# Hybrid decoder step on one core: moving the gate products of one prompt tile from the prologue of mixing into its position 0

## What is computed

```python
u = rmsnorm(x, norm_mix) @ w_in            # q, k, v | conv channels | z | a, b
o_swa = sliding-window attention with sinks (8 heads of 64, window 128)
o_gdn = chunked gated delta rule (8 heads of 64): triangular solve per chunk, state carried on
o_gdn = o_gdn * rsqrt(mean(o_gdn**2) + EPS) * gdn_norm_w * silu(z)
h = x + concat(o_swa, o_gdn) @ w_out
y = rmsnorm(h + hierarchical_moe(rmsnorm(h, norm_ffn)), norm_final)
```

## Time and profile before

| | us |
|---|---|
| median of 3 runs | 2289.5 (2286.6 to 2290.79) |
| the profiled execution, time | 2287.02 |
| the profiled execution, span | 2285.2 |
| PE busy (share of the span) | 2168.0 (95%) |
| DVE busy | 1296.6 (57%) |
| POOL busy | 612.7 (27%) |
| ACT busy | 548.6 (24%) |

### The profile page before, as it was taken

One profiled execution on the slowest core, in us unless ns is written; L12 is line 12 of the kernel. 1 busy time (PEld: TensorE's weight loads), 2 busy tenths in 40 slices (PEclk: granted clock), 3 DMA queues, 4 the chain that ended last, 5 costly groups with the idle time before them and its releaser, 6 DMA issues. The chain is left out here.

```text
span 2285.2 us, 47478 instructions
## 1 busy us (share of the span) xinstructions
PE 2168.0 (95%) x18764; PEld 1176.5 (51%) x18764; DVE 1296.6 (57%) x2674; ACT 548.6 (24%) x1421; POOL 612.7 (27%) x804
## 2 busy tenths in 40 slices
PE   7999999999988899999999999839999999999977
PEld 4444544544545666666766666524444444444433
DVE  4524425313524666556676867357767676776736
ACT  3302202202213344334434444200000001010013
POOL 1100200100200100300131221246555555555452
PEclk9999999999998899999999999959999999999988
DMA  9051040230075532233223221159999999999957
GB/s 323 20 148 38 24 148 28 51 115 13 5 206 154 134 101 70 64 86 102 75 65 117 74 65 55 58 228 357 351 373 363 370 365 379 367 383 369 346 206 307
DMA packets 171954, 405.90 MB, mean 178 GB/s; under 512 B 51188, under 2 KB 92772, under 8 KB 147162
## 3 DMA queue, kind: packets, MB, share of 16 engines
q1 hardware_dynamic: 141847, 349.34, 43.5%
q0 software_dynamic: 23648, 35.19, 4.2%
q10 hardware_dynamic: 6274, 18.72, 2.1%
HBM read 344.98 MB, written 94.80 MB: 192 GB/s over the span
## 5 line engine op out<-in xcount | busy, mean ns | idle before, releaser
L3208 PE MATMUL p_ps<-p_w_arena,k_room 128*128 128x512 f32 x1024 | 451.7, 594 | 10.8 <-DVE k_room L3110 10.8
L3208 PEld LDWEIGHTS p_ps<-p_w_arena,k_room 128*128 128x128 f32 x1024 | 195.3, 191 | 256.5 <-issue 245.5
L2864 POOL DMA_INDIRECT k_room<-s_hn,p_slot x272 | 276.4, 1016 | 123.7 <-issue 72.0
L2474 PE MATMUL p_ps<-k_room,p_mixt 128*128 128x512 f32 x544 | 263.5, 614 | 0.0
L3132 DVE STREAM_TRANSPOSE p_y_arena<-p_y_arena 32x64 f32<-32x64 f32 x1024 | 241.0, 235 | 13.2
L902 PE MATMUL p_ps<-k_room,p_w 128*128 128x512 f32 x544 | 240.6, 598 | 0.0
L902 PE MATMUL p_ps<-p_xt,p_w 128*128 128x512 f32 x544 | 238.1, 593 | 0.5 <-DVE p_xt L721 0.5
L3217 PE MATMUL p_ps<-p_w_arena,p_y_arena 128*128 128x512 f32 x512 | 231.9, 596 | 3.5 <-DVE p_y_arena L3132 3.5
L902 PEld LDWEIGHTS p_ps<-k_room,p_w 128*128 128x128 f32 x544 | 102.0, 191 | 124.1 <-issue 122.1
L902 PEld LDWEIGHTS p_ps<-p_xt,p_w 128*128 128x128 f32 x544 | 101.5, 190 | 122.6 <-issue 120.3
L3217 PEld LDWEIGHTS p_ps<-p_w_arena,p_y_arena 128*128 128x128 f32 x512 | 97.8, 191 | 127.3 <-issue 127.3
(11 more groups left out here) (442 smaller groups left out, 3002.2 us busy)
## 6 DMA issues: line engine op xcount, KB each, us to landing
p_w_arena<-in_w_exp_gate SPq DMA_DIRECT2D x64, 1024.0 KB
p_w_arena<-in_w_exp_up SPq DMA_DIRECT2D x64, 1024.0 KB
p_w_arena<-in_w_exp_down SPq DMA_DIRECT2D x64, 1024.0 KB
p_w_arena<-s_y SPq DMA_DIRECT2D x16, 1024.0 KB, 14.7
p_x<-in_x_prompt SPq DMA_DIRECT2D x30, 512.0 KB, 4.8
s_kv<-p_us SPq DMA_DIRECT2D x32, 256.0 KB
s_kq<-p_y SPq DMA_DIRECT2D x32, 256.0 KB, 3.0
p_kq<-s_kq SPq DMA_DIRECT2D x16, 512.0 KB, 5.8
```

Of the source, the lines that this page charges most:

```text
L2474: ins = mm(ps[:, 7 - n, :], mixt[t % 2][:, c, :], w_out[:, c, n * 512:(n + 1) * 512], start=(c == 0), stop=(c == KC - 1))
L2864: pool.indirect_dma_start(out=x[b][:, 256 * g:256 * g + 256], out_offset=None, in_=S["hn"].rearrange("t (q k) -> (t q) k", q=4), in_offset ...
L3208: t = mm(ps[:, 2 + b, :], xt[b][:, c, :], w_gu[bw][:, :, c, :], start=(c == 0), stop=(c == KC - 1))
```

## The change

The four pieces 12 to 15, which are the gate product of the last prompt tile (j = 3), leave the prologue. They are done in position 0 at the places where later positions have pieces 0 to 3 of the output projection. The pieces 9 to 11 now stand one each between the products and the update of the levels 1 to 3; piece 8 stays between level 0 and level 1. Tile j = 3 accumulates into bank 6 instead of 4. ACT copies and stores it after its second copy of new values in position 0, with a semaphore of its own (`gate_late`); the copies of turned probabilities that overwrite its buffer wait for that one. SP's wait for the fourth tile is left where it is.

```diff
--- before.py
+++ after.py
@@ -1290,7 +1290,7 @@
         def lg_of(t):
             return lg[:, t % 10, :]
 
-        GATE_BANK = [7, 6, 5, 4]
+        GATE_BANK = [7, 6, 5, 6]
         z_last = pt_flat.rearrange("p (j n) -> p j n", j=4)
         s_prod = oo[:].rearrange("p h d -> p (h d)").rearrange("p (c m t) -> p c m t", c=2, m=4)
         ps = ctx.psum([P, 8, 512], "ps")
@@ -1451,7 +1451,8 @@
                          on["route_in"])
                     load(route, A["c_route"][:, 0:ROUTE_MIX], on["route_in"])
                 if t == NT - 3:
-                    sp.wait_ge(on["gate_out"], 64)
+                    sp.wait_ge(on["gate_out"], 48)
+                    sp.wait_ge(on["gate_late"], 16)
                 load_window(t)
                 if t > 2:
                     load_x(t - 2)
@@ -1702,7 +1703,9 @@
                 pt_turned.after(act, t, n + 1)
                 pv_done.after(act, t - 1)
                 if t == 0:
-                    act.wait_ge(on["gate_out"], 64)
+                    act.wait_ge(on["gate_out"], 48)
+                    if n == 2:
+                        act.wait_ge(on["gate_late"], 16)
                 if t == SI + 1:
                     kdv_done.after(act, SI)
                 v, a = n // 2, n % 2
@@ -1715,7 +1718,7 @@
 
             def store_gates(j):
                 act.wait_ge(on["gate_kept"], j + 1)
-                act.dma_start(rows(S["z"], NT - 4 + j), z_last[:, j, :]).then_inc(on["gate_out"], 16)
+                act.dma_start(rows(S["z"], NT - 4 + j), z_last[:, j, :]).then_inc(on["gate_late" if j == 3 else "gate_out"], 16)
 
             def turned_mix(t):
                 mixt_turned.after(act, t)
@@ -1795,11 +1798,9 @@
             last_gates(2)
             act.wait_ge(on["invt_cleared"], 2)
             spread_inverse(0)
-            last_gates(3)
             far_copy(0)
             spread_corner(0)
-            for j in (2, 3):
-                store_gates(j)
+            store_gates(2)
             for t in range(NQ):
                 front, back, far = t + 1 < NQ, t > 0, t > 1
                 if far:
@@ -1814,6 +1815,9 @@
                     counts(PLACE_AT[t])
                 probabilities(t)
                 new_values(t)
+                if t == 0:
+                    last_gates(3)
+                    store_gates(3)
                 if far:
                     turned_hn(t - 2)
                 normalize(t)
@@ -2036,7 +2040,9 @@
                 pt_turned.after(dve, t, n + 1)
                 pv_done.after(dve, t - 1)
                 if t == 0:
-                    dve.wait_ge(on["gate_out"], 64)
+                    dve.wait_ge(on["gate_out"], 48)
+                    if n == 3:
+                        dve.wait_ge(on["gate_late"], 16)
                 v, a = n // 2, n % 2
                 nc.vector.tensor_copy(pt[:, v, :, 2 * a:2 * a + 2, :].rearrange("p c j t -> p c (j t)"),
                                       ps[:, PT_BANK[n], :].rearrange("p (c u) -> p c u", c=2)).then_inc(pt_vec.sem, 1)
@@ -2541,17 +2547,19 @@
             gate_piece(6)
             for n in range(NL):
                 level_products(0, n)
-                gate_piece(7 + 2 * n)
+                gate_piece((7, 9, 10, 11)[n])
                 level_update(0, n)
-                gate_piece(8 + 2 * n)
+                if n == 0:
+                    gate_piece(8)
             far_products(0)
-            gate_piece(15)
             far_update(0)
-            pe.wait_ge(on["gate_kept"], 4)
+            pe.wait_ge(on["gate_kept"], 3)
             pe.wait_ge(on["cleared"], 1)
             for t in range(NQ):
                 front, back, far = t + 1 < NQ, t > 0, t > 1
                 state_products(t)
+                if t == 1:
+                    pe.wait_ge(on["gate_kept"], 4)
                 scores(t, 0)
                 if front:
                     key_products(t + 1)
@@ -2566,9 +2574,15 @@
                 if back:
                     project(t - 1, 0)
                     project(t - 1, 1)
+                else:
+                    masked.after(pe, 0, 1)
+                    gate_piece(12)
+                    gate_piece(13)
                 new_values(t, 0)
                 if back:
                     project(t - 1, 2)
+                else:
+                    gate_piece(14)
                 if t in PLACE_AT:
                     counts(t)
                 if front:
@@ -2576,6 +2590,8 @@
                 new_values(t, 1)
                 if back:
                     project(t - 1, 3)
+                else:
+                    gate_piece(15)
                 if front:
                     level_products(t + 1, 0)
                 new_values(t, 2)
```

## The result

The changed kernel takes 2305.4 us (median of 4 runs, 2300.95 to 2307.83), the kernel before 2288.99 us beside it (4 runs, 2286.6 to 2290.79). The ratio is 1.0075, with a 95% interval of 1.006 to 1.009: slower by 16.4 us. The profiled execution took 2305.64 us, with a span of 2303.8 us.

A forecast was written before the change was run, and what follows sets the result against it. PE, 95% busy, bounds the kernel, with tile 2's keys having 2.2 us to spare. 12.3 + 1.1 - 0.9 = +12.5 us gives 2299.5 against the profiled 2287.0, forecast as a median of 2302; range 2295 to 2310.

The forecast's parts named there:

- Prologue: Mixing's prologue on PE: without the four gate pieces, position 0 starts 4.9 us earlier, at 716.5; bound 7.7 us.
- Release: Fourth gate tile done in position 0, freeing SP to load w_out: at 734.3 instead of 719.83, 14.5 us later.
- SP's queue: SP's time from the release to issuing tile 2's keys: 39.4 us, taken as unchanged.
- Landing: DMA of tile 2's keys and queries: lands 5.5 us after issue, at 779.2.
- Key products: PE's key products of tile 2 in position 1: at 779.2 instead of 766.93, 12.3 us later.
- Restart: PE after the stall: 1.1 us lost at the lower clock, 0.9 us won as the wait for DVE's masks goes.
- PE's lead of 1.8 us: PE from tile 1's level 1 products in position 0: 1.8 us of lead left, reaching key products at 765.1 or earlier.
- Stall: PE idle before the key products in position 1, waiting for tile 2's keys: 14 us or more.
- The store: ACT's store of the last gate tile, about 737: costed at nothing because covered, up to 5 us without cover.
- rival "faster": SP's queue drains at DMA rate, under 25.3 us, so no stall: 2283.6 us, or 2286 by the median; chance 0.07.
- rival "no change": Stall 10 us shorter because SP's one long issue, 12.93 us, hardly waits: 2292 us; chance 0.06.
- rival "lower clock over the moved pieces": Moved pieces in position 0 run at the lower clock, release up to 7.7 us later: up to 2310; chance 0.15.

The follow-up runs named there:

- run 3: Kernel before, PE's order untouched; SP's queue also waits for the second product of new values in position 0: 2297.92 us, ratio 1.0043.
- run 7: Changed kernel with only the 8 copies to the outputs moved behind the loads for tile 3: 2293.84 us, ratio 1.0043.
- run 1: Changed kernel with tile 2's keys, queries and values issued before SP waits for the fourth gate tile: 2292.43 us, ratio 1.0016.
- run 4: Changed kernel with tile 2's keys, queries and values issued right behind the weights, before the samples' inputs: 2294.91 us, ratio 1.0031.
- run 6: As run 1 on the changed kernel, plus the 8 copies to the outputs moved behind the loads for tile 3: 2287.99 us, ratio 1.0014.
- run 5: As run 1 on the changed kernel, plus SP waiting for the second level update of tile 1 before loading w_out: 2288.53 us, ratio 1.0019.

## Why the prediction was right, and where its steps were off

The sign and the mechanism hold, and the time is in the range: 2305.4, 3.4 us above the forecast of 2302. The loss itself came out larger than summed, 16.4 us in the medians and 17.8 in the profile at new values of position 1, against 12.5. By its steps:

- **Prologue**, 4.9 us won: 4.3. The half level without a piece is 1.28 us (703.17 to 704.45), as worked out. The rest is the start of the phase, where the first 12 gate records took 7.52 us instead of 6.94.
- **Release** 14.5 us later: 16.3, counted from the phase's start. That SP's row stands at 734.49, next to the 734.3 of the text, is partly luck: the phase began 1.6 us earlier in this execution, which hides a release that was 1.8 us later within it. What was undersized is the way from position 0's start to the release: 19.0 us instead of 17.8. I took the 7.2 us of the first scores and key products from the earlier trace rows; here they took 8.6, since more of them ran at the lower clock: it is 0.50 all the way from 716 to 722, and the state products at 715.49 take 3.68 us instead of 2.66. PE had been idle for 1.90 us before the far update, where a piece used to be.
- **SP's queue** 39.4 us: 39.55. **Landing** 5.5 us: 7.0; why it took longer isn't shown (5.8 in run 3, about 5.2 in run 7).
- **Key products** 12.3 us later: 15.8 (1.8 from the release, 0.2 and 1.5 from queue and landing).
- **Restart** +1.1 - 0.9: +2.0 measured (9.6 us from key products to new values instead of 7.6). With 1.8 us this term was missed by as much as the release, and it was ten times its size. The clock was 0.50 from 782 to 785, and the key products themselves lost 1.9 us, the scores 0.9. The nearest row, the start of the phase, ran at the lower clock only to 678, less than half of its 6.94 us. The relief of 0.9 us was real.
- **PE's lead of 1.8 us**, arrival at 765.1 or earlier: wrong. At the products where the text counts it (those of level 0, which it calls level 1) there was none left: they start at 734.39, 61.0 us after the phase's start, and before at 735.97, 60.9 us. PE came to the key products at 768.5, 95.1 us after the phase's start instead of 91.9. The clock did stay at 1.00 through the moved pieces and the output products (2.00 us at 737.59 instead of 3.68), but the gaps, of 6.07 us above all, took this back. I had no such term. Next to the stall it cost nothing, as PE had to wait for the keys anyway. In runs 1, 4 and 6, which have no stall, the gaps up to position 2 add up to 5.7, 6.9 and 5.0 us more than before, and these runs aren't faster than it.
- **Stall** of 14 us or more: 12.38, since PE came 5.0 us later than forecast and the keys 3.5.
- **The store** of the last gate tile, costed at nothing: issued at 737.47, landed in 11.1 us, and ACT's copy at 758.37, the first on ACT that needs it, waited for PE. The term was rightly put at nothing.
- The **rival "faster"** needed a queue under 25.3 us; it is 39.6, and without the 8 copies still 34.2 (run 7). Even without the 12.68 us of the one issue that waits for w_out it would be 26.9. Run 1 removes the stall and shows that this rival's time was wrong too: 1.0016, not 0.9985. The Trainium skill's rule that a sequencer's time for starting transfers is usually small beside them (DMA: Bandwidth & Descriptors, Issuing engines are not separate DMA queues) does not hold here: 8 loads of `s_state` alone took SP 9.98 us, and their 1.0 MB would pass in 2.5 us at the 414 GB/s of the earlier trace rows (an estimate). The **rival "no change"** wanted that one long issue to wait 10 us less: it took 12.68 us instead of 12.93. The **rival "lower clock over the moved pieces"** didn't come: they ran at 0.48 us a record.

## What to carry to other kernels

When a step is moved whose end releases a queue, follow that queue down to the first transfer with a tight due time; here it was 31 issues and 39 us behind, with 2.2 us to spare. Prefer to issue what the next position needs ahead of a wait that it has nothing to do with. Look also at which stretch of the program heavy DMA traffic falls on: where PE goes through many small products, the traffic can delay the instructions themselves.

## What the runs showed of the hardware that I had not expected

**PE has gaps with no releaser at fixed places in its program, and they end when a late packet of instructions has come.** In the changed kernel the places are after 61, 52 and 51 records of three groups of small products. Between the first two lie 3 + 64 + 8 + 52 = 127 matmul records, between the second and third 12 + 64 + 51 = 127; with as many weight loads that is 254 records each time. The kernel before has the second and third of them, shorter:

```profile
752.23 0.31 PE L2268 MATMUL p_ps<-p_inv,p_lt 32*32 32x32 f32 x12 [2.10 <-issue]
...
756.61 0.43 PE L2268 MATMUL p_ps<-p_inv,p_lt 32*32 32x32 f32 x13 [1.09 <-issue]
```

The profile's page of every run has a DMA queue of the kind "instruction":

```profile
q8 instruction: 139, 2.28, 0.4%
```

which is 16.4 KB a packet. The Trainium skill gives a matmul instruction 64 bytes (TensorE: Matmul & The Clock Gate, Part 2: What happens when you issue a matmul); by that figure a packet holds 256 instructions, close to the 254 counted.

The trace has the time of each packet, so this can be followed. In the DMA view of the changed kernel from 736.4 to 743.6 us the instruction queue is missing, and one other queue keeps the 16 engines 96.9% busy; from 743.6 to 745.1 there is one packet of it, and PE goes on at 746.31:

```profile
q1 hardware_dynamic: 409, 1.52, 96.9%
```

```profile
q8 instruction: 1, 0.02, 5.6%
```

Five gaps, in us ("place passed" is the start of PE's record at the place before the gap, about 127 records back):

| | place passed | packet | PE stops | PE goes on |
|---|---|---|---|---|
| changed, first place | 736.39 | 743.65 to 745.00 | 740.24 | 746.31 |
| run 1, first place | 736.15 | 740.67 to 742.02 | 740.00 | 743.51 |
| run 3, first place | 738.49 | 744.37 to 745.73 | 744.82 | 747.16 |
| run 5, third place | 745.13 | 752.12 to 753.46 | 748.20 | 754.99 |
| before, second place | 745.55 | 748.95 to 750.51 | 750.13 | 752.23 |

In all 48 such gaps that the twelve profiles have between 700 and 830 us, PE goes on 1.2 to 1.7 us after the end of the last instruction packet. At three places of the quiet prologue, in every profile, a packet is over 1.6 to 2.7 us after PE has passed the place; in the five rows above it takes 5.0 to 8.6 us. With w_out moved by 9 us (run 5; 6.9 us counted from the phase's start) the gap of 3.5 us at the first place vanished and one of 6.79 us came at the third. So two things set a gap's length: how late the packet is, and how soon PE needs it. The changed kernel and run 3 show the second. Their w_out starts within 0.2 us of each other and their packets come within 0.7 us, but the changed kernel's PE, at the full clock and almost without waits, is through the 128 records in 3.85 us instead of 6.3 and stops for 6.07 us instead of 2.34. In the kernel before, w_out was under way while PE needed 9.7 and 7.5 us for as many records. That the packet is late because w_out's transfers hold the DMA engines is inference from run 5 and from the busy shares.

One profile each gives the length of a gap only roughly: up to the first place run 7's program and queue are those of the changed kernel, and its gap there is 3.80 us and not 6.07. The gaps up to position 2 add up to 4.0 us in the profile before, 9.1 in the changed kernel, 9.7, 9.4 and 9.0 in runs 1, 5 and 6.
